# Attention by pairs of query tiles, with split values as stationary operand and results kept in DRAM

## The chip, the cores and the metric

The kernel runs on one core of a Trainium2 chip. The metric is the device time of one execution in microseconds. A core has five engines that run their own instruction lists and meet at semaphores: TensorE (PE: matmuls; its weight loads are shown as PEld), VectorE (DVE), ScalarE (ACT), GpSimd (POOL) and SyncE (SP, which here only issues transfers). Matmul results go to PSUM, eight banks of 128 partitions by 512 f32; everything else stands in SBUF.

## The reference, cut to what matters

One encoder layer over 2048 tokens of width 1024. The change touches the attention head group (8 heads) and how its result reaches the output projection. All is float32.

```python
q_rope = rope(q[..., 64:], cos, sin);  k_rope = rope(k_r, cos, sin)        # k_rope shared by the heads
s = einsum('bqhd,bkhd->bhqk', qn, k_nope) + einsum('bqhr,bkr->bhqk', qr, k_rope)
mask = key_chunk[None, :] <= q_chunk[:, None]                              # chunks of 64 tokens
p = softmax(where(mask, s * scale, -inf))
out = einsum('bhqk,bkhd->bqhd', p, v)                                      # (tokens, 8 heads x 64)
...
a = rms_norm(out, mla_out_g);  r = hgrn2_group(...)
h = layer_norm(ALPHA * x + concat([a, r]) @ w_out)
# then a mixture of 32 experts and a second layer norm
```

## The kernel before, in words

The program is a sequence of stages with a barrier between them: constants (phase_0), input projection and recurrence (phase_a), attention (phase_b), output projection with the first layer norm and router logits (phase_c), routing, experts, and the last layer norm. Within a stage every engine has a hand-written list, and semaphores with counted values set the order.

**Attention (phase_b, lines 639 to 870).** A loop over four pairs of heads (`pairs`, line 676); the first pass is written out, the other three are a hardware loop. A pass has two parts. First, twenty projections (`PREP`, line 672): k and q of both heads in four column chunks, and v in four. TensorE projects into the four S banks (lines 718, 721, 725), ScalarE copies k, the upper half of q, and v to SBUF (793, 795, 797), VectorE multiplies the rotary half of q by the trigonometric table (830). No attention work stands beside this part.

Then 32 items, one query tile of 128 rows for one head each (`ITEMS`), small and large tiles alternating. An item has q+1 key tiles, hence 1 to 4 banks (`BANKS`) of up to 512 scores. Its steps:
- scores, one f32 matmul per bank (769); an f32 matmul of these leaves two records in the trace
- row maximum per bank (845) with the masked corner written first (843), then over the banks (847), then negated and scaled (849), on VectorE
- exponential with the row sum accumulated (808), on ScalarE
- transposes of the probabilities, 128x128 each, up to four into one of two T banks (741); even banks are copied to SBUF by VectorE (859), odd ones by ScalarE (819)
- values: for each key tile one matmul with the transposed probabilities as stationary and 64 columns of v as moving operand (753)
- VectorE divides by the row sum and writes to `ao` in SBUF (865, 867, 870)

TensorE runs three items deep: in one turn it writes the scores of item n, then, group by group, the transposes of item n-1 and the values of item n-2. Nothing in a group's copy has to be ready before the next turn.

**Output projection (phase_c).** Eight steps of two token tiles. At the start of each step VectorE copies the next two tiles' attention results out of `ao` (`pick`, line 1113); ScalarE squares, sums and normalises them (1044 to 1054), TensorE transposes them into a single bank (985), ScalarE casts that to the rounded form `anT_hi` (1061), and VectorE subtracts to get the remainder `anT_lo` (1121).
## Time and profile before

| | us |
|---|---|
| median of 3 runs | 2902.32 (2900.85 to 2907.87) |
| the profiled execution | 2898.33 |
| its span | 2896.5 |
| TensorE / VectorE / ScalarE / GpSimd busy | 2587.7 / 1547.9 / 1076.9 / 308.8 |
| mean granted TensorE clock | 0.949 |

By stage (from the span's start): up to 823 us input projection and recurrence; 823 to 1618 attention; 1618 to 1872 output projection; then routing, experts from about 1985 to 2800, and the last norm. Busy time is the union of an engine's records. TensorE's are pipelined and their ends modelled, so a record is longer than its turn: how long a matmul holds TensorE is read from the distance between the starts of records that follow each other without a gap. The granted clock is the share of 2.4 GHz that TensorE was given; it has two levels, full and half. Where a line of the profile says `<-ACT pr L808 10.2`, the engine stood idle for 10.2 us in all until ScalarE's line 808 released it.

### The profile page before, as it was taken

To read this page: it belongs to the slowest core of one execution; us is meant where nothing else is said; L and a number is where in the kernel's file an instruction comes from. 1 tells how busy PE (TensorE), PEld (TensorE's weight loads), DVE (VectorE), ACT (ScalarE), POOL (GpSimd) and SP (SyncE) were. 2 spreads that over 40 slices of the span, in tenths; PEclk is the share of its full clock that TensorE was granted. 3 is DMA by queue.
4 is the path that set the end of the run, shared out by engine and by line. 5 is a ranking of instruction groups with operands and counts; after the bars stand their busy time and mean duration, and the time that the engine had idled before them with its cause. 6 is when DMAs were issued, how large, how long until landed. Compare 5 with 4: busy or idle time off the path is not lost. (4 is left out here: it accounts for less than half of the span.)

```text
span 2896.5 us, 42439 instructions
## 1 busy us (share of the span) xinstructions
PE 2587.7 (89%) x13160; PEld 2034.3 (70%) x13161; DVE 1547.9 (53%) x2657; ACT 1076.9 (37%) x1711; POOL 308.8 (11%) x221
## 2 busy tenths in 40 slices
PE   5999999999979999999989799937999999999960
PEld 4887788778837767667667578726877788888850
DVE  3334433343236546546456455465878775655738
ACT  2122222222134444344444322105666555545533
POOL 0000000000000000000000011100323332222215
PEclk9999999999979999999999899958999999999985
DMA  5000000000010000000000222257999997786935
GB/s 195 1 22 22 22 0 22 22 22 0 8 35 1 1 6 1 2 6 1 2 1 1 95 94 72 80 171 287 371 328 373 311 344 242 240 302 221 307 95 232
DMA packets 129115, 330.11 MB, mean 114 GB/s; under 512 B 7137, under 2 KB 19041, under 8 KB 128737
## 3 DMA queue, kind: packets, MB, share of 16 engines
q1 hardware_dynamic: 115904, 281.06, 26.4%
q0 software_dynamic: 13104, 47.72, 6.7%
q8 instruction: 57, 0.93, 0.1%
q14 instruction: 50, 0.40, 0.0%
HBM read 284.19 MB, written 53.48 MB: 117 GB/s over the span
## 5 line engine op out<-in xcount | busy, mean ns | idle before, releaser
L1582 DVE TENSOR_TENSOR w_raw<-w_raw,w_hi 128x4096 f32 (+1 forms) x96 | 424.5, 4422 | 149.2 <-ACT w_hi L1573 149.0
L1573 ACT CAST w_hi<-w_raw 128x4096 fp32r (+1 forms) x96 | 347.2, 3635 | 104.8 <-DMA w_raw<-in_w 93.8
L312 PE MATMUL pa<-xT,wi 128*128 128x256 f32 (+1 forms) x1536 | 335.6, 380 | 0.0
L808 ACT ACTIVATE pr<-pS,nmx 128x512 f32<-128x512 f32 (+3 forms) x320 | 195.7, 620 | 338.7 <-DVE nmx L849 328.0
L312 PEld LDWEIGHTS pa<-xT,wi 128*128 128x128 f32 (+1 forms) x1536 | 283.7, 186 | 53.9 <-issue 9.6
L1522 PE MATMUL eH<-w_hi,xh 128*128 128x512 f32 x720 | 290.6, 404 | 15.1 <-DVE xl L1640 15.1
L1523 PE MATMUL eH<-w_hi,xl 128*128 128x512 f32 x720 | 286.8, 398 | 0.0
L769 PE MATMUL pS<-kT,qT 128*128 128x512 f32 (+3 forms) x640 | 260.7, 539 | 12.2 <-ACT pr L808 8.4
L753 PE MATMUL pO<-vp,prT 128*128 128x64 f32 x2176 | 264.9, 271 | 0.0
L753 PEld LDWEIGHTS pO<-vp,prT 128*128 128x128 f32 x2176 | 259.6, 193 | 1.2 <-issue 1.2
L1092 POOL TENSOR_TENSOR hp<-hp,b 128x1024 f32<-128x1024 f32 x16 | 40.9, 2554 | 1812.0 <-DVE hp L1155 1812.0
L741 PE MATMUL pT<-ident,pr 128*128 128x128 f32 x1088 | 183.9, 291 | 42.4 <-ACT prT L819 25.2
L845 DVE TENSOR_REDUCE mx<-pS 128x1 f32<-128x512 f32 (+3 forms) x320 | 192.9, 609 | 45.5 <-PE pS L769 39.6
L741 PEld LDWEIGHTS pT<-ident,pr 128*128 128x128 f32 x1088 | 138.5, 155 | 87.9 <-ACT prT L819 25.6
L769 PEld LDWEIGHTS pS<-kT,qT 128*128 128x128 f32 x640 | 112.6, 193 | 108.7 <-issue 86.6
L1527 PE MATMUL eH<-w_raw,xh 128*128 x720 | 184.3, 398 | 4.6 <-DVE w_raw L1582 4.5
L1522 PEld LDWEIGHTS eH<-w_hi,xh 128*128 128x128 f32 x720 | 136.7, 190 | 47.5 <-issue 15.0
L1527 PEld LDWEIGHTS eH<-w_raw,xh 128*128 128x128 f32 x720 | 134.9, 188 | 40.2 <-issue 8.5
L601 DVE SCALAR_TENSOR_TENSOR state<-state,gf,pu 128x128 f32<-128x128 f32 x256 | 71.8, 342 | 164.4 <-PE po L425 146.2
L1541 PE MATMUL eY<-w_hi,uh 128*128 128x512 f32 x360 | 147.5, 410 | 13.0 <-ACT w_hi L1573 13.0
L1523 PEld LDWEIGHTS eH<-w_hi,xl 128*128 128x128 f32 x720 | 136.9, 190 | 31.3
L859 DVE COPY prT<-pT 128x512 f32<-128x512 f32 (+3 forms) x160 | 99.9, 624 | 88.4 <-PE pT L741 87.6
(271 smaller groups left out, 3873.5 us busy)
## 6 DMA issues: line engine op xcount, KB each, us to landing
w_raw<-in_w SPq DMA_DIRECT2D x96, 2048.0 KB, 13.1
xt<-in_x SPq DMA_DIRECT2D x8, 1024.0 KB, 5.6
wi<-in_w_in SPq DMA_DIRECT2D x4, 2048.0 KB, 17.3
xs<-in_x SPq DMA_DIRECT2D x8, 1024.0 KB, 4.9
scratch_h<-hp SPq DMA_DIRECT2D x16, 512.0 KB, 2.7
fz<-scratch_z SPq DMA_DIRECT2D x16, 512.0 KB, 9.7
out<-fz SPq DMA_DIRECT2D x16, 512.0 KB, 2.6
scratch_rT<-ot SPq DMA_DIRECT2D x8, 512.0 KB, 3.2
```

Of the source, the lines that this page charges most:

```text
L312: ins = pe.matmul(B[b][0:m_cols, 0:SPAN], wi[:, k, col:col + m_cols], xT[:, k, :], start=(k == 0), stop=(k == KT - 1))
L741: ins = pe.transpose(TB[u % 2][:, i * P:(i + 1) * P], pr[:, n % 2, kt_ * P:(kt_ + 1) * P], t["ident"][:])
L753: ins = pe.matmul(OB[n % 2][:, 0:VD], prT[:, n % 2, kt_, :], vp[:, kt_, x * VD:(x + 1) * VD], start=(kt_ == 0), stop=(kt_ == q))
L769: pe.matmul(S[u % 4][:, 0:w], qT[:, x, q * P:(q + 1) * P], kT[:, x, j * 512:j * 512 + w], start=True, stop=True).then_inc(s_done, 1)
L808: nc.scalar.activation(pr[:, n % 2, j * 512:j * 512 + w], S[u % 4][:, 0:w], ACT.Exp, scale=SCALE, bias=nmx[:, n:n + 1], accum_out=rsum[:, ...
L845: v.tensor_reduce(mx[:, n, j:j + 1], S[u % 4][:, 0:w], AX, ALU.max).then_inc(mx_part, 1)
L1522: pe.matmul(H[:], xh[:, k, :], w.hi[:, k, :], start=(k == 0), stop=False)
L1523: pe.matmul(H[:], xl[:, k, :], w.hi[:, k, :], start=False, stop=False)
L1527: ins = pe.matmul(H[:], xh[:, k, :], lo[:, k, :], start=False, stop=(k == KT - 1))
L1541: pe.matmul(Y[half][:], uh[:, k, :], w2.hi[:, k, at], start=(k == 0), stop=False)
L1573: nc.scalar.copy(w.hi[:], w.words(o).bitcast(F32)).then_inc(w.hi_ready, 1)
L1582: v.tensor_tensor(w.words(o), w.words(o).bitcast(F32), w.hi[:].bitcast(F32), ALU.subtract).then_inc(w.lo_ready, 1)
```

## The change

Attention is written anew. It now walks over 64 steps (`STEPS_B`): head by head, and in a head over eight pairs of query tiles, upward in even heads and downward in odd ones. Nothing is a loop any more; all is written out. A step has two halves, one for each query tile of the pair.
- q, k and v are kept as hi and lo. Scores are three split matmuls per bank (`score`).
- v's hi and lo stand side by side, 64 and 64 columns, as the stationary operand; the transposed probabilities of both query tiles, cast to hi by ScalarE (`cast`) and subtracted to lo by VectorE (`rest`), are the moving operand of 256 columns. A unit is two key tiles by two query tiles: four transposes into a bank and four matmuls (`weigh`), four units later (`LAG`), from a ring of six.
- The sum over a pair comes out as a transposed 128x256 block, the hi half over the lo half. ScalarE copies it (`copy_o`), and a small f32 matmul with a stacked identity both adds the halves and turns it back (`fold`), into one of the same two T banks. VectorE divides (`divide`), and SyncE stores it to DRAM.
- The projections of the next head are spread over pairs 0 to 3 of this one (`prep_in`), one chunk of k or q or v in a half. The rotary half of q now waits for ScalarE's copy of the upper half; then ScalarE casts the whole and VectorE subtracts.
- In the output projection, `pick` is gone: SyncE loads two tiles' attention results from DRAM, for the next step at the start of each. The norm's gain and bias are loaded there and no longer during attention.

```diff
+LAG, RING, FOLD_LAG = 4, 6, 2
...
+def prep_in(n, i):
+    h, q = STEPS_B[n]
+    if q > 3 or h + 1 == HEADS:
+        return []
...
-                                pe.matmul(S[u % 4][:, 0:w], qT[:, x, q * P:(q + 1) * P], kT[:, x, j * 512:j * 512 + w],
-                                          start=True, stop=True).then_inc(s_done, 1)
+                        pe.matmul(b[:, 0:w], qh[:, x, at], kh[:, x, keys], start=True, stop=False)
+                        pe.matmul(b[:, 0:w], ql[:, x, at], kh[:, x, keys], start=False, stop=False)
+                        pe.matmul(b[:, 0:w], qh[:, x, at], kl[:, x, keys], start=False, stop=True).then_inc(scored, 1)
...
+                def free_turn(e):
+                    if e >= NTB:
+                        kind, who = T_ORDER[e - NTB]
+                        if kind == "unit":
+                            pe.wait_ge(t_lo, who + 1)
+                        else:
+                            pe.wait_ge(a_ready, who + 1)
+                    return T[e % NTB]
...
-                            ins = pe.matmul(OB[n % 2][:, 0:VD], prT[:, n % 2, kt_, :], vp[:, kt_, x * VD:(x + 1) * VD],
-                                            start=(kt_ == 0), stop=(kt_ == q))
+                    for m, (kk, w) in enumerate(((0, ph), (1, ph), (1, pl), (0, pl))):
+                        narrow = kk == 1 and g == q
+                        o = out[:, P:2 * P] if narrow else out
+                        at = slice(2 * P, 3 * P) if narrow else slice(kk * 2 * P, (kk + 1) * 2 * P)
+                        ins = pe.matmul(o, v[:, 2 * g + kk], w[:, u % RING, at], start=(g == 0 and m == 0), stop=(g == q and m == 3))
...
+                def fold(n):
+                    pe.wait_ge(o_copied, n + 1)
+                    b = free_turn(T_AT["fold", n])
+                    for i in range(2):
+                        ins = pe.matmul(b[:, i * VD:(i + 1) * VD], oT[:, n % 2, i * P:(i + 1) * P], t["fold"][:, 0:VD], start=True, stop=True)
...
+                for n in range(NI + 2):
+                    for i in range(2):
+                        if n < NI:
+                            score(n, i)
+                            for p in prep_in(n, i):
+                                project(p)
+                        for s in slots_in(n, i):
+                            if s < NU:
+                                turn(s)
+                            if LAG <= s < NU + LAG:
+                                weigh(s - LAG)
+                            if s in FOLD_SLOT:
+                                fold(FOLD_SLOT[s])
...
+                        for k in range(max(len(slots), pieces)):
+                            if k < len(slots):
+                                if slots[k] < NU:
+                                    cast(slots[k])
+                                if slots[k] in COPY_SLOT:
+                                    copy_o(COPY_SLOT[slots[k]])
+                            if k < pieces:
+                                exp(n, i, k)
+                            if k == 0 and n < NI:
+                                for p in prep_in(n, i):
+                                    copy_q(p) if p[0] == "q" else split(p)
...
+                        if n < NI:
+                            peak(n, i)
+                            for p in prep_in(n, i):
+                                rope(p) if p[0] == "q" else split(p)
+                        for s in slots_in(n, i):
+                            if s < NU:
+                                rest(s)
+                            if s in FOLD_SLOT:
+                                divide(FOLD_SLOT[s])
...
 # phase_c
+                sp.dma_start(ap[:], ad[0]).then_inc(a_loaded, 16)
...
+                    if not last:
+                        sp.wait_ge(a_norm, m * 2 + 2)
+                        sp.dma_start(ap[:], ad[m + 1]).then_inc(a_loaded, 16)
...
-                    v.tensor_scalar(ap[:], t["ao"][:, bass.ds(m * 2, 2), :], 1.0, None, ALU.mult).then_inc(a_picked, 1)
...
-                    if not last:
-                        pick(m + 1)
```

TensorE's list before, at an item of two banks between a larger and a smaller one (pS scores, pT transposes, pO values):

```order
L769 MATMUL pS<-kT,qT 128x512
L769 MATMUL pS<-kT,qT 128x384
L741 MATMUL pT<-ident,pr 128x128 x4
L753 MATMUL pO<-vp,prT 128x64 x4
L741 MATMUL pT<-ident,pr 128x128 x4
L753 MATMUL pO<-vp,prT 128x64 x2
L741 MATMUL pT<-ident,pr 128x128 x3
```

and now, in a large pair, the last score matmul of one half, its first and last unit, and the next half's first scores (k_hi and k_lo, q_hi and q_lo, prT_hi and prT_lo are the parts of the split):

```order
L825 MATMUL pS<-k_lo,q_hi 128x384
L843 MATMUL pT<-ident,pr 128x128 x4
L863 MATMUL pO<-prT_hi,v_split 128x256 x2
L863 MATMUL pO<-prT_lo,v_split 128x256 x2
...
L843 MATMUL pT<-ident,pr 128x128 x4
L863 MATMUL pO<-prT_hi,v_split 128x256
L863 MATMUL pO<-prT_hi,v_split 128x128
L863 MATMUL pO<-prT_lo,v_split 128x128
L863 MATMUL pO<-prT_lo,v_split 128x256
L823 MATMUL pS<-k_hi,q_hi 128x512
L824 MATMUL pS<-k_hi,q_lo 128x512
```

Scores are three matmuls where one stood, and a half's units stand behind its scores, each with four transposes and, for an earlier unit, four wide value matmuls.

VectorE's list before, for one item of four banks (mx, mxa, nmx the maxima; rsa, rin the row sums):

```order
L845 TENSOR_REDUCE mx<-pS 128x1 x3
L843 MEMSET pS 64x64
L845 TENSOR_REDUCE mx<-pS 128x1
L847 TENSOR_REDUCE mxa<-mx 128x1
L849 TENSOR_SCALAR nmx<-mxa 128x1
L859 COPY prT<-pT 128x384
L865 TENSOR_REDUCE rsa<-rsum 128x1
L867 RECIPROCAL rin<-rsa 128x1
L870 TENSOR_SCALAR ao<-pO,rin 128x64
```

and now, for a half of a small pair in which q and v of the next head are projected, and the maxima of the half behind it:

```order
L1016 TENSOR_REDUCE mxa<-mx 128x1
L1018 TENSOR_SCALAR nmx<-mxa 128x1
L985 TENSOR_TENSOR q_raw<-pS,trig 64x512
L1002 TENSOR_TENSOR v_split<-pS,v_split 128x4x64 x2
L1023 TENSOR_TENSOR prT_lo<-pT,prT_hi 128x512
L1023 TENSOR_TENSOR prT_lo<-pT,prT_hi 128x384
L994 TENSOR_TENSOR q_lo<-q_raw,q_hi 128x512
L1014 TENSOR_REDUCE mx<-pS 128x1
L1012 MEMSET pS 64x64
L1014 TENSOR_REDUCE mx<-pS 128x1
L1016 TENSOR_REDUCE mxa<-mx 128x1
L1018 TENSOR_SCALAR nmx<-mxa 128x1
```

Between one half's maxima and the next's stand the subtraction of every unit (prT_lo), and around these the rotary product, v's remainder and q's remainder. ScalarE's list alternates a unit's cast with an exponential, and the pieces of the next head stand behind the first exponential of a half.

In the output projection, VectorE at the border of two steps before:

```order
L1117 TENSOR_TENSOR rts_lo<-rts,rts_hi 128x512
L1101 COPY hT<-cH 128x512
L923 UNCONDITIONAL_BRANCH
L923 ISA
L1113 ISA
L1113 TENSOR_SCALAR ap<-ao 128x1024
L1120 ISA
L1121 TENSOR_TENSOR anT_lo<-cA,anT_hi 128x512
```

and now:

```order
L1342 TENSOR_TENSOR hp<-hp,g 128x1024
L1306 TENSOR_TENSOR rts_lo<-rts,rts_hi 128x512
L1296 COPY hT<-cH 128x512
L1111 UNCONDITIONAL_BRANCH
L1111 ISA
L1310 TENSOR_TENSOR anT_lo<-cA,anT_hi 128x512
```

The copy `ap<-ao` between the last copy of a step and the first anT_lo of the next is gone.

## Rows read from the trace of the kernel before

**Rows 1.** The page: engines' busy time; one row of its transfers.
```profile
PE 2587.7 (89%) x13160; PEld 2034.3 (70%) x13161; DVE 1547.9 (53%) x2657; ACT 1076.9 (37%) x1711; POOL 308.8 (11%) x221
...
scratch_h<-hp SPq DMA_DIRECT2D x16, 512.0 KB, 2.7
```

**Rows 2.** Busy by stretch: PE, PEld, DVE, ACT, POOL, granted clock, DMA share, GB/s.
```profile
858.00:1050.00 192.00, 178.53 (x1036) 130.09 (x1037) 107.03 (x320) 80.27 (x219) 0.00 (x0) 0.97 0.01 3
...
1240.00:1430.00 190.00, 173.94 (x1044) 128.24 (x1042) 104.72 (x318) 78.77 (x217) 0.00 (x0) 0.98 0.01 4
```

**Rows 3.** Who waited for whom, 860 to 1610: total us, times, longest.
```profile
ACT pr L808 <- DVE nmx L849: 325.4, 116, 5.7
```

**Rows 4.** Groups by shape, attention: busy us, mean ns, idle before and releasers.
```profile
L753 PE MATMUL pO<-vp,prT 128*128 128x64 f32 x2176 | 264.9, 271 | 0.0
...
L769 PE MATMUL pS<-kT,qT 128*128 128x512 f32 x448 | 213.8, 603 | 0.0
L741 PE MATMUL pT<-ident,pr 128*128 128x128 f32 x1088 | 183.9, 291 | 42.4 <-ACT prT L819 25.2 <-ACT pr L808 10.2 <-DVE prT L859 6.7
```

**Rows 5.** Timelines of TensorE: start, length of the run, records (x).
```profile
706.93 1.99 PE L320 MATMUL pa<-xT,wi 128*128 128x256 f32 x8
...
839.99 14.00 PE L721 MATMUL pS<-cqn,wq 128*128 128x512 f32 x32
853.83 3.73 PE L725 MATMUL pS<-wv,ckvn 128*128 128x128 f32 x32
...
1204.00 0.60 PE L741 MATMUL pT<-ident,pr 128*128 128x128 f32 x4
1204.43 1.00 PE L753 MATMUL pO<-vp,prT 128*128 128x64 f32 x8
```

**Rows 6.** Timeline of TensorE in the experts: split matmuls.
```profile
1999.81 0.40 PE L1542 MATMUL eY<-w_hi,ul 128*128 128x512 f32 x1
2000.04 0.40 PE L1541 MATMUL eY<-w_hi,uh 128*128 128x512 f32 x1
```

**Rows 7.** Timeline of VectorE and ScalarE, an item of two banks.
```profile
1209.29 0.69 DVE L845 TENSOR_REDUCE mx<-pS 128x1 f32<-128x512 f32 x1
1210.01 0.15 DVE L847 TENSOR_REDUCE mxa<-mx 128x1 f32<-128x2 f32 x1
1210.20 0.15 DVE L849 TENSOR_SCALAR nmx<-mxa 128x1 f32<-128x1 f32 x1
...
1210.39 0.69 ACT L808 ACTIVATE pr<-pS,nmx 128x512 f32<-128x512 f32 x1 [2.67 <-DVE nmx L849]
...
1211.07 0.68 ACT L808 ACTIVATE pr<-pS,nmx 128x512 f32<-128x512 f32 x1
...
1212.76 1.31 DVE L845 TENSOR_REDUCE mx<-pS 128x1 f32<-128x512 f32 x2
```

**Rows 8.** Timeline of ScalarE at the start of attention: two copies.
```profile
825.30 1.06 ACT L785 COPY kT<-pS 64x512 f32<-64x512 f32 x2 [15.19 <-PE pS L703]
```

**Rows 9.** Busy by stretch, end of the output projection.
```profile
1850.00:1900.00 50.00, 36.21 (x186) 31.45 (x184) 20.90 (x44) 5.82 (x12) 7.52 (x3) 0.79 0.28 101
```

**Rows 10.** Output projection: timeline around one step's start; its wait in total.
```profile
1703.10 2.18 DVE L1113 TENSOR_SCALAR ap<-ao 128x1024 f32 x1
...
1705.20 0.68 DVE L1121 TENSOR_TENSOR anT_lo<-cA,anT_hi 128x512 fp32r<-128x512 f32 x1
1706.03 0.63 PE L985 MATMUL cA<-ident,an 128*128 128x128 f32 x4 [1.68 <-DVE anT_lo L1121]
...
PE cA L985 <- DVE anT_lo L1121: 14.3, 7, 3.5
```

**Rows 11.** Timeline of the output projection's first load and the cast it releases.
```profile
1618.66 0.39 SPq L930 DMA_DIRECT2D rts<-scratch_rT  x1
...
1622.20 1.14 ACT L1031 CAST rts_hi<-rts 128x512 fp32r<-128x512 f32 x2 [5.89 <-DMA rts<-scratch_rT]
```

More of the change, by code:

```diff
@@ L116, in shape_constants @@
     fold[:64, 64:] = (s[:64, None] % 32 == s[None, :64] % 32)
+    fold[:, :64] = (s[:, None] % 64 == s[None, :64])
     c["fold"] = fold
@@ L639, in phase_b @@
+S_ORDER = bank_order()
+S_AT = {e: n for n, e in enumerate(S_ORDER)}
+T_ORDER = [e for s in range(SLOTS + 1) for e in ([("unit", s)] if s < NU else []) + ([("fold", FOLD_SLOT[s])] if s in FOLD_SLOT else [])]
+T_AT = {e: n for n, e in enumerate(T_ORDER)}
+NTB = 2
 def phase_b(nc, t, d):
@@ new lines, in phase_b @@
+        qraw = sb("q_raw", [P, 2, 512])
+        pr = [t["krp"]] + [sb(f"pr{i}", [P, SEQ]) for i in range(3)]
+        ph = sb("prT_hi", [P, RING, 512], F32R); pl = sb("prT_lo", [P, RING, 512], F32R)
+        oT = sb("oT", [P, 2, 2 * P])
+        a = sb("a_out", [P, 4, 2, VD])
+        mx = sb("mx", [P, 4, 4])
+        mxa = sb("mxa", [P, 2 * NI])
+        nmx = sb("nmx", [P, 2 * NI])
+        rsum = sb("rsum", [P, 2 * NI, 4])
+        rin = sb("rin", [P, 2 * NI])
+        S = [psum(f"pS{i}") for i in range(4)]
@@ new lines, in peak @@
+                def peak(n, i):
+                    tile, pieces, part = 2 * n + i, PIECES[n][i], EXP_AT[n][i]
+                    for j in range(pieces):
+                        b, w = S[S_AT["score", (n, i, j)] % 4], width(n, i, j)
+                        v.wait_ge(scored, part + j + 1)
+                        if j == pieces - 1:
+                            v.memset(b[0:64, w - 64:w], -3.0e38).then_inc(masked, 1)
+                            v.wait_ge(masked, tile + 1)
+                        v.tensor_reduce(mx[:, tile % 4, j:j + 1], b[:, 0:w], AX, ALU.max).then_inc(mx_part, 1)
+                    v.wait_ge(mx_part, part + pieces)
+                    v.tensor_reduce(mxa[:, tile:tile + 1], mx[:, tile % 4, 0:pieces], AX, ALU.max).then_inc(mx_all, 1)
+                    v.wait_ge(mx_all, tile + 1)
+                    v.tensor_scalar(nmx[:, tile:tile + 1], mxa[:, tile:tile + 1], -SCALE, None, ALU.mult).then_inc(nmx_ready, 1)
```

468 lines of the change are left out of this document (269 added, 199 removed).

## The prediction

> **What bounds the kernel now.** I read the page first, then the stages, then the attention stage (lines 703 to 870) by shapes and waits. The profiled execution took 2898.3 us, 1.8 more than its span; the median of the runs is 2902.3, so what I add to the one I add to the other. TensorE is busy 89% of the span, VectorE 53%, ScalarE 37% [rows 1]. The change touches two stages: attention, from 823 to about 1618 us, 795 us long, and the output projection behind it, to about 1872 [rows 2]. In one of attention's four head pairs TensorE's records cover 174 of 190 us, VectorE's 105, ScalarE's 79 [rows 2]. ScalarE waits 325 us for the negated maximum [rows 3], while TensorE's largest wait, before transposes, is 42 us in all [rows 4].
>
> TensorE's own work there goes by the distance from one record to the next, not by their length, since records overlap [rows 5]: an f32 matmul leaves two records, of 0.432 us at 512 columns (31 distances in 14.00-0.59), 0.229 at 256, 0.112 at 128 and 0.107 at 64; a transpose leaves one, 0.11 us. With the counts of the shapes (the three largest in [rows 4]; the others follow from the loops):
> - scores 448x0.432 + 64x(0.325+0.229+0.112) = 236 us (0.325 for 384 columns lies between its neighbours)
> - probabilities times values 2176x0.107 = 233
> - transposes 1088x0.11 = 120
> - projections 128x0.432 + 64x0.432 + 128x0.112 = 97, rotary fold 6
>
> That is 692 us of 795; the other 103 are waits, gaps and low clock.
>
> **What the change makes of that work.** Each score piece becomes three split matmuls. A warm split matmul of 512 columns follows the next after 0.23 us, 0.234 over the longer run they stand in [rows 6]; none narrower is in the trace. Bounds for 256 columns: half the distance, 0.117, and the f32 pair, 0.458. I take 0.127, the row's 0.020 over its streaming kept, because the row is the same kind of instruction. For 384 I take 0.18; for 128 the bounds are 0.06 and 0.224, and I take 0.22, the f32 row of that very width, on the side of caution (it moves the sum by 35 us at most).
> - scores 672x0.234 + 96x(0.18+0.127+0.22) = 208 (was 236)
> - values: 288 units of four matmuls, of which 128 have 128 columns: 1024x0.127 + 128x0.22 = 158 (was 233)
> - transposes 120, projections 97, rotary fold 6: as before
> - new: 128 folds of hi and lo, f32, 64 columns, 2x0.107 each = 27
>
> Sum 616: TensorE is relieved of 76 us. The bounds of the unknown widths (for 384, up to the f32 pair's 0.65) make this 570 to about 1030.
>
> The other two pay. Before, 160 groups of probabilities were copied by VectorE and 160 by ScalarE. Now each of 288 units is cast by ScalarE and then subtracted by VectorE: 128 more casts at about 0.53 and 128 more VectorE passes at about 0.62. Also new are the hi and lo of q, k and v. VectorE's sum goes from some 430 (four pairs like those of [rows 2]) to about 560, ScalarE's from 330 to 480. Neither becomes the bound by its sum; the order is what costs.
>
> **The new waits.** Turned probabilities have only two PSUM banks and each unit's bank is freed by the second engine in series. I follow the rounds, one round being half a pair of query tiles. VectorE's step costs in a chain: 0.62 per 512 piece, then mask, last reduction, mxa and nmx 0.15+0.72+0.19+0.19 = 1.25; exp to exp 0.68 [rows 7]; copies back to back 0.48 for two of 0.58 in 1.06 us [rows 8], 0.53 for casts; the next engine starts about 0.03 after a record's end, TensorE 0.15 after (1705.88 to 1706.03 in [rows 10]).
> - Long rounds (pairs 4 to 7, 64 of them). With four pieces and four units: scores 4x3x0.234 = 2.81, first transposes 0.63 until seen, cast 0.53, exp 0.68, cast 0.59, subtraction 0.69, 0.15 to TensorE, fourth transposes 0.44, values 0.51: 7.03. Once per pair ScalarE's copy of O and VectorE's division (0.15+0.17+0.28 and their own gaps) stand in this chain, 0.45 per round: 7.5. TensorE's work in it with its share of folds is 6.8. Over the 64, TensorE's work is 5.6 on average (18.6 scores, 24.7 units, 1.7 folds per head, by eight rounds); I add 0.9: 6.55x64 = 419.
> - Short rounds that project a piece of k for the next head (28): VectorE's circle is peak 1.55 (half a 0.62, and 1.25), exp 0.71, ScalarE's k_hi 0.58, 0.03, k_lo 0.69, subtractions 0.80, division 0.4: 4.8, against some 3.1 of TensorE. 134.
> - Those that project q (16): 1.55, 0.71, copy 0.51, rotary product 0.72, subtractions 0.80, q_lo 0.62, division 0.6: 5.5, 88. With v as well (12): two casts and two subtractions of 256 columns and 0.9 of projection more, 8.0, 96.
> - Short rounds of the last head (8) 3.2 each, 26; rotary fold and head 0's twelve projections 27; the end 5.
>
> Sum 795 us: the waits grow from 103 to 179 and eat TensorE's relief exactly. What hid the copies before, a whole query tile of scores and values between a transpose and its use, has become four units.
>
> **The clock.** Attention was granted 0.97 and 0.98 in the pairs shown [rows 2]. At the end of the output projection, with records over 36 of 50 us and longer pauses, it was 0.79 [rows 9]. A share of 0.88 means that a quarter of the time passes at 1.2 instead of 2.4 GHz. With 616 us of work in 795, I estimate 0.88 in place of 0.97. TensorE's links are 4.4 of a 7.5 us chain, so 250 us of the long rounds plus 20 at the start stretch by a tenth: +25, between 0 and the 60 of a clock of 0.79. By the Trainium skill, TensorE: Matmul & The Clock Gate, Part 4 on PE-mode transposes, transposes do not count as TensorE activity in the same way as matmuls. By that, the 120 us of transposes, now a larger part of less work, help the clock less than the records suggest; no row here separates them. With that rule the term lies nearer 60 than 0.
>
> **The ends.** The results go to DRAM, and the stage waits for the last store: a 512 KB store lands in 2.7 us [rows 1], so +3; the other 63 stores have nobody behind them but the same output buffer four pairs later. The output projection loses its copy of attention results out of SBUF, 2.18 us of VectorE in the loop. It stood between the end of a step and anT_lo, for which TensorE waited 14.3 us in 7 steps [rows 10]: -13. The new load of the next two tiles waits on SyncE behind the store of the tile before, a few us into a step, and lands some 3.5 us later (as rts does, 1618.66 to 1622.20 in [rows 11]), and the normalisation is wanted at the next step, some 20 us later: hidden. SyncE's queue gets a_norm in front, which is a step old by then. The first load stands behind rts, whose landing starts the stage: up to 1 us more. The gain and bias loads move behind x, used only after the last wo_lo, about 1642: hidden.
>
> **Sum.** Profiled: 2898.3 + (795-795) + 25 + 3 - 13 = 2913; as a median, 2917 us, 0.5% slower.
>
> **Rivals.**
> - Even. The clock holds at 0.97 (the pauses are single microseconds): 2917-25 = 2892. For it: pauses of this length stand in attention now, with 0.97. Against it: there are more of them.
> - Faster: the rounds overlap better than my chains. TensorE runs up to its LAG of four units ahead, so that waits stay at today's 103: attention 719, total 2902-76-13+3 = 2816; with half of that 2860. For it: TensorE is the fullest engine, and every other sum is below 616. Against it: two banks, not six ring slots, limit the transposes, and every q passes ScalarE, VectorE, ScalarE, VectorE.
> - Slower: the weight loads of the split matmuls show. An f32 matmul of 64 columns takes 0.107 per record, though its share of the 512-column row is 0.054 [rows 5], so loads do bound narrow ones. If at 256 columns a load of some 0.10 stood beside the stream, 0.207 each: 1024x0.080 = +82 of work, of which the loops' idle 0.9 a round absorbs a third: 2917+55 = 2972. It decides from the point where the 256-column distance passes 0.14. A clock of 0.8 throughout gives about 2950 by another way. The Trainium skill, same page, section on LDWEIGHTS, puts a load at columns over 1.2, in ns: an estimate of 107 ns for 128 columns, just what streaming 256 columns takes here, so hiding is just possible by it.
> - Split matmuls under 512 columns run at the f32 pair's speed: 1120x0.331 = 371 more work, and the waits hide a fourth of it at most: near 3200.
>
> **How the numbers follow.** A difference under 0.3%, 9 us, is what measuring can't tell from none. My forecast, 2895 to 2945, has 0.37: faster 0.03, same 0.08, slower 0.26. Even, 0.25: 0.12, 0.10, 0.03. Faster, 0.25, all faster. Slower, 0.10, and the f32 speed, 0.03, all slower. Sum: faster 0.40, same 0.18, slower 0.42. The range leaves out the f32 speed and half of the faster rival: 2835 to 2975.
>
> **What would show it.** Attention's length, 795 now: 820 forecast. Per step: the distance of 256- and 128-column split matmuls; TensorE's idle time before transposes ended by VectorE's prT_lo, and before scores ended by ScalarE's exp; rounds of 7.5 us in pair 7 and 5 to 8 in pairs 0 to 3; the granted clock; no wait of cA for anT_lo. It is wrong if TensorE's waits for prT_lo and exp stay near today's, if the clock stays at 0.97, or if VectorE is seen working without a gap.

## The result

The changed kernel takes **2921.0 us**, the median of 7 runs (2913.8 to 2924.8); the kernel before took 2902.6 us (7 runs, 2899.0 to 2907.9). The ratio is 1.0057, with a 95% interval of 1.0041 to 1.0073: slower by 18 us, 0.6%. The forecast was 2917 us, in a range of 2835 to 2975. The profiled execution took 2924.2 us, 2922.4 of them its span, against 2898.3 before.

The two changed stages can be bounded by events: attention begins with TensorE's first matmul of the stage, at 823.3 us before and at 825.7 now, and SyncE issues the output projection's first load when attention's results have been stored. (The words ahead of the prediction let the output projection end near 1872; TensorE's last matmul for the logits, cL, starts at 1890.1.)

```profile
825.73 7.06 PE L774 MATMUL pS<-krp,fold 64*64 64x512 f32 x8 [13.94 <-PEq L630]
```

| | before | after | forecast of the difference |
|---|---|---|---|
| all ahead of attention (unchanged code) | 823.3 us | 825.7 us | 0 |
| attention, from there to that load | 795.3 us (to 1618.66) | 811.9 us (to 1637.59) | +28 |
| output projection, to the last cL | 271.4 us (to 1890.1) | 268.8 us (to 1906.4) | -13 |
| all that follows (unchanged code) | 1008 us | 1018 us | 0 |
| profiled execution | 2898.3 | 2924.2 | +15 |

The 2.4 us ahead of attention and the last 10 us belong to no edit: the text of the stages there is the same. Most of it is the scatter of single executions: in the traces of the experiments below, attention began between 822.8 and 829.1 us, and all that follows took 1005 to 1017 us. The profile of before also lies 4 us under the median of its kernel, and that of after 3 us over. For the change itself +16.5 and -2.6 us remain, 14 of the 18.4 us between the medians.

### The profile page after: what moved, and what is told of

The parts are those of the page before. It is cut to its first block and busy times, and to the rows that moved or that the text cites. A ratio compares the mean times of both kernels' runs of the same rounds, so it can differ in the third digit from the quotient of the medians.

```text
span 2922.4 us, 41381 instructions
## 1 busy us (share of the span) xinstructions
PE 2533.2 (87%) x12712; PEld 2028.5 (69%) x12713; DVE 1640.9 (56%) x2690; ACT 1184.5 (41%) x1951; POOL 317.2 (11%) x221
## 5 line engine op out<-in xcount | busy, mean ns | idle before, releaser
L935 ACT CAST prT_hi<-pT 128x512 fp32r<-128x512 f32 (+1 forms) x288 | 161.9, 562 | 264.9 <-PE pT L843 264.9
L1023 DVE TENSOR_TENSOR prT_lo<-pT,prT_hi 128x512 fp32r<-128x512 f32 (+1 forms) x288 | 187.7, 656 | 100.0 <-ACT prT_hi L935 99.8
L1014 DVE TENSOR_REDUCE mx<-pS 128x1 f32<-128x512 f32 (+2 forms) x320 | 188.8, 607 | 16.8 <-PE pS L825 10.9
L843 PE MATMUL pT<-ident,pr 128*128 128x128 f32 x832 | 158.2, 283 | 37.6 <-DVE prT_lo L1023 36.2
L927 ACT ACTIVATE pr<-pS,nmx 128x512 f32<-128x512 f32 (+1 forms) x240 | 153.3, 641 | 53.0 <-DVE nmx L1018 50.4
L843 PEld LDWEIGHTS pT<-ident,pr 128*128 128x128 f32 x832 | 104.6, 146 | 65.5 <-issue 41.7
L1729 PE MATMUL eY<-w_hi,ul 128*128 128x512 f32 x360 | 144.1, 400 | 0.0
L823 PE MATMUL pS<-k_hi,q_hi 128*128 128x512 f32 (+2 forms) x320 | 129.1, 403 | 13.2 <-ACT pr L927 11.2
L863 PE MATMUL pO<-prT_hi,v_split 128*128 128x256 f32 x576 | 138.6, 323 | 0.0
## 6 DMA issues: line engine op xcount, KB each, us to landing
fz<-scratch_z SPq DMA_DIRECT2D x16, 512.0 KB, 10.7
```

The source lines that it names most:

```text
L843: ins = pe.transpose(b[:, m * P:(m + 1) * P], probs(n, i)[:, kt * P:(kt + 1) * P], t["ident"][:])
L927: nc.scalar.activation(probs(n, i)[:, j * 512:j * 512 + w], S[S_AT["score", (n, i, j)] % 4][:, 0:w], ACT.Exp, scale=SCALE, bias=nmx[:, til ...
L935: nc.scalar.copy(ph[:, u % RING, 0:w], T[T_AT["unit", u] % NTB][:, 0:w]).then_inc(t_hi, 1)
L1014: v.tensor_reduce(mx[:, tile % 4, j:j + 1], b[:, 0:w], AX, ALU.max).then_inc(mx_part, 1)
L1023: v.tensor_tensor(pl[:, u % RING, 0:w], T[T_AT["unit", u] % NTB][:, 0:w], ph[:, u % RING, 0:w].bitcast(F32), ALU.subtract).then_inc(t_lo, 1)
```

## The profile after

The page of the changed kernel, busy time and share first; then three groups (busy us, mean ns, idle time before them and who ended it). It answers to [rows 1] and [rows 4].

```profile
PE 2533.2 (87%) x12712; PEld 2028.5 (69%) x12713; DVE 1640.9 (56%) x2690; ACT 1184.5 (41%) x1951; POOL 317.2 (11%) x221
...
L935 ACT CAST prT_hi<-pT 128x512 fp32r<-128x512 f32 (+1 forms) x288 | 161.9, 562 | 264.9 <-PE pT L843 264.9
L1023 DVE TENSOR_TENSOR prT_lo<-pT,prT_hi 128x512 fp32r<-128x512 f32 (+1 forms) x288 | 187.7, 656 | 100.0 <-ACT prT_hi L935 99.8
...
L843 PE MATMUL pT<-ident,pr 128*128 128x128 f32 x832 | 158.2, 283 | 37.6 <-DVE prT_lo L1023 36.2
```

TensorE has 448 records less and is 54 us less busy, VectorE 93 us more, ScalarE 108 us more. The waits have changed hands. Before, ScalarE waited 325 us for the negated maximum [rows 3]; now its largest wait is for transposes, and TensorE's largest is for the subtraction. (Two names, pr and krp, stand for the buffers of probabilities in these rows: one of the four buffers is the tile that held the rotary part of k.) The view of who waited for whom, 825 to 1600 us (total, times, longest):

```profile
ACT prT_hi L935 <- PE pT L843: 256.1, 138, 7.0
DVE prT_lo L1023 <- ACT prT_hi L935: 92.8, 147, 1.3
DVE q_raw L985 <- ACT q_raw L917: 79.9, 32, 5.1
...
PE pT L843 <- DVE prT_lo L1023: 60.7, 89, 2.6
ACT pr L927 <- DVE nmx L1018: 47.0, 54, 2.8
...
DVE k_lo L997 <- ACT k_hi L906: 36.1, 28, 2.1
```

With the wait ahead of the folds (30.2 us in 36, of the same releaser), TensorE waits 91 us for VectorE's remainder; before, its waits for the copies that empty a turn bank came to 25.2 + 6.7 us [rows 4]. This is a circle: a turn bank is filled by four transposes, cast by ScalarE, subtracted from by VectorE, and only then free, and there are two such banks.

The pitch of the split matmuls, which the forecast had to bound, is read from starts. Three stretches of TensorE's timeline: score pieces of 512 and 384 columns, of 128, and one unit with its first and last transpose, its four value matmuls and the next unit's first transpose:

```profile
1332.64 0.39 PE L825 MATMUL pS<-k_lo,q_hi 128*128 128x512 f32 x1
1332.87 0.33 PE L823 MATMUL pS<-k_hi,q_hi 128*128 128x384 f32 x1
1333.04 0.34 PE L824 MATMUL pS<-k_hi,q_lo 128*128 128x384 f32 x1
...
1157.74 0.22 PE L823 MATMUL pS<-k_hi,q_hi 128*128 128x128 f32 x1
1157.80 0.28 PE L824 MATMUL pS<-k_hi,q_lo 128*128 128x128 f32 x1
1157.91 0.28 PE L825 MATMUL pS<-k_lo,q_hi 128*128 128x128 f32 x1
...
1340.68 0.27 PE L843 MATMUL pT<-ident,krp 128*128 128x128 f32 x1
...
1341.00 0.27 PE L843 MATMUL pT<-ident,pr 128*128 128x128 f32 x1
1341.03 0.48 PE L863 MATMUL pO<-prT_hi,v_split 128*128 128x256 f32 x2
1341.35 0.40 PE L863 MATMUL pO<-prT_lo,v_split 128*128 128x256 f32 x2
1341.59 0.27 PE L843 MATMUL pT<-ident,krp 128*128 128x128 f32 x1
```

So 512 columns take 0.23 us, 384 take 0.17, and 128 take 0.11, half of the 0.22 assumed. Only the first of three 128-column matmuls, behind one of 512, is followed sooner, after 0.06 (1157.74 to 1157.80). 256 columns take 0.11 to 0.12 (three starts at 1164.59, 1164.70 and 1164.82). A whole unit, four transposes and four value matmuls, takes 0.91 us (1340.68 to 1341.59); the first value matmul follows the last transpose after 0.03 us, and the third follows the first after 0.32.

Where the clock is low is seen by stretches (PE, PEld, DVE, ACT, POOL, clock, DMA share, GB/s). Each cycle of two heads has a long part, large pairs, and a short part, in which the next head's q, k and v are made. The first row is a long part, the second a short one; the bounds are starts of VectorE's divisions, a_out:

```profile
1102.00:1195.00 93.00, 82.84 (x558) 72.91 (x557) 70.22 (x163) 61.00 (x160) 0.00 (x0) 1.00 0.04 11
1195.00:1306.00 111.00, 84.61 (x385) 58.43 (x384) 60.74 (x164) 46.20 (x120) 0.00 (x0) 0.85 0.02 5
```

The 0.97 of before [rows 2] has become 1.00 in the long part and 0.85 in the short one. What the engine did before it fell, in such a short part (timeline; in brackets the idle time before, and who ended it):

```profile
1076.56 0.44 PE L863 MATMUL pO<-prT_lo,v_split 128*128 128x128 f32 x2
1079.67 1.27 DVE L1023 TENSOR_TENSOR prT_lo<-pT,prT_hi 128x512 fp32r<-128x512 f32 x2
1080.49 1.09 PE L870 MATMUL pT<-fold,oT 128*128 128x64 f32 x4 [3.48 <-DVE prT_lo L1023]
...
1082.76 0.63 PE L823 MATMUL pS<-k_hi,q_hi 128*128 128x512 f32 x1
1083.19 0.63 PE L824 MATMUL pS<-k_hi,q_lo 128*128 128x512 f32 x1
...
1094.23 1.09 PE L843 MATMUL pT<-ident,pr 128*128 128x128 f32 x4 [2.33 <-DVE prT_lo L1023]
```

TensorE stood 3.5 us for the remainder, and the matmuls behind it follow each other after 0.43 us instead of 0.23: that is the level of 1.2 GHz, and a pause is paid twice. It needs none of the longest: only three of TensorE's pauses in attention exceed 3 us, and behind the 2.33 us before 1094.23 the transposes are slow as well (four in 1.09 us, 0.63 at the full clock).

For the experiments one row of each kernel suffices, the whole of attention. Before and after:

```profile
825.00:1616.00 791.00, 730.35 (x4215) 528.28 (x4214) 425.21 (x1276) 329.02 (x888) 0.00 (x0) 0.97 0.02 5
```

```profile
825.00:1635.00 810.00, 673.28 (x3784) 522.92 (x3784) 532.00 (x1320) 435.56 (x1129) 0.00 (x0) 0.92 0.03 8
```

The part in which no matmul record runs grew from 61 to 137 us (791-730, 810-673). In later rows the same 3784 matmuls cover less time at a higher clock, so such a row parts a gain into pauses (the difference of the first two numbers) and, in the main, clock (the second number). Not all of the second number is clock: between the kernel with three edits and the last run it falls from 634 to 615 us at the same 0.98.

## The experiments

**Theory T**: the added waits come from the circle through two turn banks, with the rotary product of q and its clock as a second loss and the new load of attention's results as a third. **R1**: TensorE's work, or other waits, set the time, and a third bank adds little.

### Three turn banks

The eight PSUM banks are divided into 4 for scores, 3 for turned probabilities and 1 for outputs, in place of 4, 2 and 2; a pair's first value matmul then waits for the copy of the pair before.

```
-NTB = 2
+NTB = 3
...
-        O = [psum(f"pO{i}")[:, 0:2 * P] for i in range(2)]
+        O = [psum("pO")[:, 0:2 * P]] * 2
...
-                    if g == 0 and n >= 2:
-                        pe.wait_ge(o_copied, n - 1)
+                    if g == 0 and n >= 1:
+                        pe.wait_ge(o_copied, n)
```

> The changed kernel with three PSUM banks for turned probabilities instead of two; the bank is taken from the output sums, which now share one. Theory (T): attention's lost time is the wait for the second engine in series to free one of two banks. In the changed kernel TensorE waits 63 us before transposes and 31 us before folds for VectorE's prT_lo, 94 in all, and ScalarE waits 265 us for transposes. With a third bank most of the 94 go and some of it is taken back by other waits: attention 812 -> 750 to 765 us, total 2921 -> 2865 to 2880, TensorE's wait for prT_lo under 30 us. Rival (R1, engines' work): VectorE and ScalarE are simply loaded with more; the order of banks does not matter: total within 9 us of 2921. Rival (R2, clock): the low clock of 0.92 is the cause, the banks only through it: total falls by less than 25 us and only where the clock rises.

Measured: 2833.6 us (2826.8 to 2837.3), ratio to the kernel before 0.9759 (0.9745 to 0.9773), 87 us less than the changed kernel, and more than either reading expected. Attention as a whole, then its long and short part:

```profile
825.00:1550.00 725.00, 643.11 (x3781) 498.41 (x3780) 523.62 (x1318) 432.37 (x1129) 0.00 (x0) 0.96 0.04 9
...
1071.00:1158.00 87.00, 82.81 (x559) 72.40 (x559) 69.48 (x167) 60.60 (x162) 0.00 (x0) 1.00 0.05 12
1158.00:1249.00 91.00, 73.82 (x389) 49.86 (x388) 60.26 (x165) 46.25 (x121) 0.00 (x0) 0.98 0.03 7
```

and TensorE's wait for the remainder (825 to 1600):

```profile
PE pT L848 <- DVE prT_lo L1028: 11.7, 24, 0.8
```

Attention is 85 us shorter: 55 of it pauses (137 to 82) and 30 the same matmuls at the higher clock (673 to 643). The wait ahead of transposes fell from 60.7 to 11.7 us, its longest from 2.6 to 0.8, and the one ahead of folds from 30.2 to 1.2. The long part loses 6 us of 93, the short part 20 of 111. The expectation had the pauses about right; theory T left out the clock, and R2, which named it, allowed less than 25 us.

### One output bank alone

The same, with the two turn banks kept: this parts the third turn bank from what was given up for it.

> Control for the run with three banks: the changed kernel with the output sums in one bank and the turned probabilities still in two. A pair's first value matmul must then wait for ScalarE's copy of the pair before. Theory T: this costs up to 10 us and gains nothing, 2921 to 2931. If the run with three banks gained because of something else in that edit, this one would gain as well.

Measured: 2919.3 us (2915.1 to 2923.4), ratio 1.0053 (1.0037 to 1.0069). No difference from the changed kernel: the whole 87 us belong to the third turn bank.

### The rotary product of q without its wait

VectorE's product of q with the cosines waited for ScalarE's copy of q's other half, which is needed only by the cast behind both. The wait is moved to that cast.

```
-                    v.wait_ge(q_copied, Q_AT[m] + 1)
                     v.tensor_tensor(qraw[64:128, ...], S[...][64:128, :], t["trig"][64:128, ...], ...)
...
+                        act.wait_ge(q_copied, Q_AT[m] + 1)
                         act.wait_ge(q_roped, Q_AT[m] + 1)
```

> The changed kernel with VectorE's rotary product no longer waiting for ScalarE's copy of q's upper half (the cast of the whole q waits for both). In the changed kernel VectorE stood 79.9 us before this product in 32 places. Theory T (short rounds are a chain ScalarE, VectorE, ScalarE, VectorE): the product moves in front of the copy and half a microsecond of each of the 28 chains goes, with the exponential before it in some: 10 to 30 us less, 2891 to 2911. Rival R1 (the wait covers TensorE's projection anyway): under 6 us, VectorE then waits for the projection instead.

Measured: 2885.0 us (2878.3 to 2886.4), ratio 0.9933 (0.992 to 0.9945), 36 us less than the changed kernel, more than the 10 to 30 expected. Attention, then its long and short part:

```profile
825.00:1600.00 775.00, 646.90 (x3783) 506.56 (x3781) 531.79 (x1319) 435.11 (x1129) 0.00 (x0) 0.96 0.03 8
...
1087.00:1180.00 93.00, 82.84 (x558) 72.84 (x557) 70.31 (x163) 60.98 (x160) 0.00 (x0) 1.00 0.04 11
1180.00:1281.00 101.00, 76.52 (x385) 52.91 (x383) 60.57 (x163) 45.79 (x119) 0.00 (x0) 0.93 0.03 6
```

VectorE's wait for that copy is gone; a part of it comes back further on, since its wait ahead of v's remainder grew from 12.1 to 41.8 us. The long part is untouched, as it must be, since no q is made there; the short part is 10 us shorter. Of the 35 us that attention lost, only 9 are pauses (137 to 128) and 26 are clock (673 to 647). An edit that takes single microseconds out of a few pauses was worth almost four times that, and most of it is the engine's higher level.

### The load one tile earlier

In the output projection, the load of the next two tiles of attention results waits behind the store of the tile before. It is issued ahead of that store instead, late in the step before.

```
-                    if not last:
-                        sp.wait_ge(a_norm, m * 2 + 2)
-                        sp.dma_start(ap[:], ad[m + 1]).then_inc(a_loaded, 16)
...
+                            if more:
+                                sp.wait_ge(a_norm, m * 2 + 4)
+                                sp.dma_start(ap[:], ad[m + 2]).then_inc(a_loaded, 16)
```

> The changed kernel with the output projection's load of attention results issued half a step earlier on SyncE, ahead of the store of the second tile. In the changed kernel ScalarE waited 27.6 us for this load in 7 steps, VectorE's reciprocal 37.5 us behind it, and the reciprocal stands in VectorE's list before the residual sum; TensorE still waited 10.7 us for anT_lo. Theory T: that late load is where the predicted 13 us went: 8 to 12 us less, TensorE's wait for anT_lo under 3 us, ScalarE's wait for the load near 0. Rival: TensorE's own work bounds the step and the load is hidden: within 3 us, anT_lo still waited for.

Measured: 2913.1 us (2904.3 to 2917.5), ratio 1.0036 (1.0023 to 1.005), 8 us less, at the lower edge of the 8 to 12 expected; the interval still overlaps the changed kernel's, so the trace has to decide. First the changed kernel; this step of the output projection begins at 1723.7, with VectorE's anT_lo:

```profile
1726.39 0.37 SPq L1133 DMA_DIRECT2D ap<-scratch_a  x1
...
1730.02 0.63 ACT L1238 ACTIVATE an<-ap 128x512 f32<-128x512 f32 x1 [4.23 <-DMA ap<-scratch_a]
...
1731.86 0.17 DVE L1315 RECIPROCAL ars<-ars 128x2 f32<-128x2 f32 x1 [5.34 <-ACT ars L1243]
...
1732.14 1.28 DVE L1330 SCALAR_TENSOR_TENSOR hp<-xs,cM 128x512 f32<-128x512 f32 x2
```

The load is issued 2.7 us into the step and is used 3.6 us later. In ScalarE's list the normalisation for the next step stands right behind this step's two casts, done at 1725.8, so ScalarE waits for it from then on, VectorE's reciprocal (ars) waits for ScalarE, and the residual sum (hp), for which TensorE's results had been ready, stands behind the reciprocal in VectorE's list. With the early load (issued at 1720.08) ScalarE's wait falls from 27.6 us in 7 to 0.6 in 1, and the stage takes 262.1 us (1639.97 to 1902.1) against 268.8. TensorE's wait for anT_lo is 6.2 us in 2, not the under 3 that was expected.

### All three

> The changed kernel with all three edits: three banks for transposed probabilities and one for outputs, the rotary half without its wait, the output projection's load issued one tile earlier. Theory T (three separate losses: the turn banks 87 us, the rotary multiply 36, the load 8, the first two sharing a part of the rising clock): 2785 to 2815 us, waits of TensorE in attention under 80 us, clock there 0.96 to 0.98. Rival R1 (the banks' gain already holds the rotary's, since both filled the same idle time): 2820 us or more.

Measured: 2806.8 us (2799.8 to 2811.3), ratio 0.9667 (0.9652 to 0.9682), 114 us less than the changed kernel and 3.3% under the kernel before; alone the three gave 87, 36 and 8. Attention:

```profile
825.00:1529.00 704.00, 633.75 (x3783) 492.81 (x3781) 524.22 (x1319) 431.66 (x1129) 0.00 (x0) 0.98 0.04 9
```

So this run's rival falls, though of the rotary edit's 36 us only some 19 (114-87-8) come on top of the banks'. The pauses are down to 70 us, near those of the kernel before (61), for less work.

### One score matmul instead of three

```
-                        pe.matmul(b[:, 0:w], qh[:, x, at], kh[:, x, keys], start=True, stop=False)
-                        pe.matmul(b[:, 0:w], ql[:, x, at], kh[:, x, keys], start=False, stop=False)
-                        pe.matmul(b[:, 0:w], qh[:, x, at], kl[:, x, keys], start=False, stop=True).then_inc(scored, 1)
+                        pe.matmul(b[:, 0:w], qh[:, x, at], kh[:, x, keys], start=True, stop=True).then_inc(scored, 1)
```

> Each score bank gets one matmul instead of three (the two with a remainder are left out), everything else as in the changed kernel; about 125 us of TensorE's attention work is gone. Theory T (rounds last as long as the chain copy, subtraction, value matmuls, next turn on two banks): most of it turns into waiting, 5 to 40 us less than the changed kernel, 2880 to 2916 us. Rival R2 (TensorE's work sets the attention): 100 us less or more, 2820 us or below.

Measured: 2901.9 us (2894.9 to 2905.0), ratio 1.0002 (0.9993 to 1.0011). A sixth of the stage's matmuls, 640, are left out, and the kernel gains 19 us:

```profile
825.00:1617.00 792.00, 582.62 (x3143) 433.42 (x3141) 527.04 (x1319) 436.36 (x1129) 0.00 (x0) 0.88 0.03 8
...
1094.00:1188.00 94.00, 71.19 (x462) 60.87 (x462) 70.24 (x167) 61.20 (x161) 0.00 (x0) 0.93 0.04 11
```

The pauses grew from 137 to 209 us and the clock fell from 0.92 to 0.88. The long part lasts 94 us with one matmul for a piece, and 93 with three. TensorE's amount of work, though it is the fullest engine of the page, does not set the length of attention in the changed kernel.

### No remainders of the probabilities

VectorE's subtraction is left out, and the two value matmuls that use its result; a turn bank is free after the cast.

```
-                            pe.wait_ge(t_lo, who + 1)
+                            pe.wait_ge(t_hi, who + 1)
...
-                    for m, (kk, w) in enumerate(((0, ph), (1, ph), (1, pl), (0, pl))):
+                    for m, (kk, w) in enumerate(((1, ph), (0, ph)) if g else ((0, ph), (1, ph))):
```

> The remainders of the transposed probabilities are left out: no subtraction on VectorE (188 us busy) and two of the four value matmuls of each unit (about 70 us of TensorE work), everything else as in the changed kernel. Theory T (the subtraction stands in the loop that holds a turn bank): 100 to 160 us less, 2760 to 2820 us, more than the run with one score matmul although less TensorE work is gone. Rival R2 (TensorE's work sets the attention): 50 to 75 us less, 2845 to 2870 us, and less than that run gains.

Measured: 2779.6 us (2776.7 to 2780.6), ratio 0.9573 (0.9559 to 0.9588): 141 us less, with 576 matmuls fewer, each narrower than most of the 640 of the run above. Set beside it, this says which work lies in the circle: with the subtraction out as well, less TensorE work removed buys seven times as much. The run alone doesn't part a bank that is free sooner from a VectorE that has less to do; the third bank, with VectorE's work unchanged, does.

### The kernel before with three turn banks

Does the old kernel gain by the same division of banks? It too had two turn banks, each emptied by one copy of one engine.

```
-        TB = [psum(f"pT{i}") for i in range(2)]
-        OB = [psum(f"pO{i}") for i in range(2)]
+        TB = [psum(f"pT{i}") for i in range(3)]
+        OB = [psum("pO")] * 2
...
```

> The kernel before with the same division of banks: three for transposed probabilities, one for outputs. Its two turn banks are each emptied by one copy of one engine, without a subtraction. Theory T (the rewrite made the loop through a turn bank long; before it was short): 0 to 25 us less than the kernel before, 2878 to 2903 us, so that the rewrite is worth 40 us or more once both have three banks. Rival R3 (two turn banks held back the kernel before as much): 50 us less or more, 2850 us or below.

Measured: 2875.9 us (2869.8 to 2877.4), ratio 0.9903 (0.9887 to 0.9918), 25 us less than before, at the edge of the 0 to 25 expected; its attention takes 768.2 us (829.06 to 1597.22) instead of 795.3, 27 less. With three turn banks on either side the rewrite is the faster kernel, by 42 us (2833.6 to 2875.9); with two it is the slower one, by 18.

### The wait for the remainder moved behind the first two value matmuls

```
-                    pe.wait_ge(t_lo, u + 1)
                     for m, (kk, w) in enumerate(((0, ph), (1, ph), (1, pl), (0, pl))):
+                        if m == 2:
+                            pe.wait_ge(t_lo, u + 1)
```

> As the run with all three edits (2807 us), but TensorE begins a unit's two value matmuls with the rounded probabilities when the copy is there, and waits for VectorE's remainder only ahead of the other two. With three turn banks the wait ahead of a unit's value matmuls is the first that needs this unit's remainder, so it can move. Theory T: what is left of TensorE's waits for the remainder shrinks, 5 to 25 us less, 2782 to 2802 us. Rival R4 (TensorE's own work and the softmax's passes now set the attention): 2800 to 2814 us.

> The same later wait put into the changed kernel as it is, with two turn banks. Theory T (the turn that stands ahead of a unit's value matmuls reuses this unit's bank, so it has already waited for the same remainder): no difference, 2913 to 2926 us. Rival R1 (the value matmuls' own wait costs the time, not the bank): 15 us less or more, 2906 us or below.

Measured: 2808.0 us (2801.6 to 2809.4) in the kernel with three edits, nothing gained, as R4 said and against T; and 2919.3 us (2911.2 to 2921.7) in the changed kernel, ratio 1.0051 (1.0033 to 1.0069), no difference, as T said. The wait ahead of the value matmuls is never the late one: the wait before transposes is 11.7 us in 24 in the run with three edits and in this one alike. So something else holds up what is left.

### What is left: one score matmul, and a shorter maximum

> One score matmul instead of three (the two with a remainder are left out) in the kernel with all three edits. With two turn banks this was worth 19 us. Theory T (with the waits gone TensorE's work and its clock set more of the attention): 40 to 90 us less than the 2807 of the same kernel with three, 2717 to 2767 us. Rival R5 (the attention still hangs on the engines' chains, and less work only lowers the granted clock): under 30 us less, 2777 us or above.

Measured: 2814.6 us (2809.6 to 2822.5), ratio 0.9706 (0.9681 to 0.9731). Theory T failed: nothing is gained. Attention:

```profile
825.00:1538.00 713.00, 556.60 (x3143) 410.54 (x3141) 524.44 (x1320) 430.93 (x1129) 0.00 (x0) 0.93 0.04 9
```

TensorE's wait for a score bank, 825 to 1500, here and in the run with the three edits and all three matmuls:

```profile
PE pS L825 <- ACT pr L931: 50.6, 81, 1.6
```

```profile
PE pS L825 <- ACT pr L933: 10.6, 26, 1.0
```

The work taken from TensorE turned into waiting for the exponential that frees a score bank, and the clock fell from 0.98 to 0.93. This points to a second circle: score bank, maximum, negated maximum, exponential, bank free. The last run shortens VectorE's pass in it:

```
-                        v.tensor_reduce(mx[:, tile % 4, j:j + 1], b[:, 0:w], AX, ALU.max).then_inc(mx_part, 1)
+                        v.tensor_reduce(mx[:, tile % 4, j:j + 1], b[:, 0:64], AX, ALU.max).then_inc(mx_part, 1)
```

> The kernel with all three edits (2807 us), but VectorE's pass over a score bank takes its maximum from the first 64 columns only: the same instructions in the same order, some 0.45 us shorter each, 320 of them, about 140 us of VectorE in attention. A softmax needs no exact maximum, so the computation stands but for its safety with large scores. Theory C (what is left, also with one score matmul, is the circle score bank, maximum, negated maximum, exponential, bank free again): 40 to 110 us less, 2700 to 2767 us. Rival R6 (TensorE's work, whose records cover 634 of 704 us, sets the attention): under 30 us less, 2777 us or above.

Measured: 2755.7 us (2750.9 to 2756.4), ratio 0.9498 (0.9482 to 0.9514), 51 us less than the kernel with three edits, and the fastest that was run. Its maxima, as a group, and then its attention by the view of stretches:

```profile
L1019 DVE TENSOR_REDUCE mx<-pS 128x1 f32<-128x64 f32 x320 | 68.1, 220 | 27.2 <-PE pS L827 22.7
```

```profile
825.00:1480.00 655.00, 615.22 (x3783) 491.49 (x3781) 412.36 (x1320) 424.81 (x1129) 0.00 (x0) 0.98 0.04 10
```

118 us less of VectorE (186 to 68) shortened attention by 50 us, while a sixth of TensorE's matmuls less had shortened it by nothing. The result lies where theory C had it. VectorE also frees the turn banks, and it has 118 us less to do in all, so this run does not part a shorter circle of score banks from an earlier subtraction or a less loaded VectorE: C is supported, not shown, and that stays open.

## Why the prediction was nearly right, point by point

- **TensorE's work, 616 us.** Some 34 us too high. The 128-column score pieces take 0.11, not 0.22: 96 x 0.11 = 11 us less. In back-to-back units (0.91 us) the four transposes and four value matmuls cost 0.04 less than the 0.95 assumed, over 288 units another 11. The 128 narrow value matmuls, put at 0.22 against 0.127 for wide ones, take no longer than these: 12 more. About 582 us at full clock, an estimate. The guess for 256 columns, 0.127, was the one on which most hung (1024 matmuls), and it held within 0.01 to 0.02.
- **The rival of unhidden weight loads, 2972, and that of f32 speed, near 3200.** Both are out: the first decided from a pitch above 0.14 at 256 columns, and the rows have 0.11 to 0.12. The narrow matmuls do show a floor, 0.11 us for 128 columns as for 256 where they follow one another. The Trainium skill (TensorE: Matmul & The Clock Gate, section on LDWEIGHTS) puts a load at the columns over 1.2, in ns, an estimate of 107 ns for 128. The trace agrees with that page, and not with the rival, which let the load stand beside the stream.
- **The waits grow and eat the relief.** Right in mechanism, and shown by experiment: the third turn bank returned 87 us, the giving up of an output bank nothing. The prediction named it, "two banks, not six ring slots, limit the transposes", as what speaks against the faster rival. A long round of four pieces was to last 7.5 us; scores start at 1330.71 and those of the next half at 1337.93, 7.2 us. The sizes are less right. Attention's 812 us less the 582 of work leave 230 us of waits, gaps and low clock, where the forecast had 207 (179, 25 and 3). Work too high by 34 and waits too low by 23 partly cancel inside one term. The other two engines' work was overstated as well: VectorE had 532 us in attention against 560, ScalarE 436 against 480.
- **The clock.** +25 us for 0.88; measured 0.92. The same matmuls cover 673 us at 0.92, 643 at 0.96 and 634 at 0.98 (three edits), so against the 0.97 of before the clock costs some 35 us, an estimate. The size was near; the place was wrong. The prediction put the stretch on the long rounds, which ran at 1.00. It falls in the short ones (0.85), behind pauses like those of 2.33 and 3.48 us above. The long rounds ran at 1.00 though up to four transposes stand in every unit of 0.91 us, so nothing here bears out the rule of the Trainium skill (same page, Part 4) on transposes, by which the prediction would have moved the term towards 60.
- **The ends of attention.** The last result is divided out at 1635.1 and the load goes at 1637.59: 2.5 us, against 0.5 before (1618.11 to 1618.66), when nothing had to be stored: +2, near the forecast (3).
- **The output projection, -13, measured -2.6.** This is the step that failed: "the normalisation is wanted at the next step, some 20 us later: hidden." That the load goes a few us into a step was right (2.7). But the next step's normalisation is wanted early in the same step, 0.6 us before the load is even issued, and in VectorE's list its reciprocal stands ahead of the residual sum. The wait that was to vanish (14.3 us in 7, [rows 10]) is 10.7 us in 8. The early load gets 6.7 us of it back (268.8 to 262.1), and with it the stage is 9.3 us shorter than before, near the 13 of the forecast.
- **The sum.** +15 forecast for the profiled execution, +26 measured, +14 of it in the changed stages: attention 11.5 us better than the +28, the output projection 10 us worse than the -13. Two misses of opposite sign, and a third pair inside attention: the closeness of 2917 to 2921 is in good part luck.
- **The even rival, 2892, and the faster one, 2816 or 2860.** The clock did not hold, so the first is out. The second describes a kernel one edit away: with three turn banks the pauses fall to 82 us and the time to 2834. What decides between it and the forecast could have been read ahead: a turn bank is held for its transposes, 0.44, the cast, 0.56, and the subtraction, 0.66, in series, 1.66 us without the hand-overs; by two banks 0.83 per unit, only 0.08 under TensorE's 0.91, which the hand-overs take (to TensorE alone the prediction had 0.15 per unit, by two banks 0.08); by three 0.55.

## What to carry to other kernels

When a second engine is put in series on a buffer, count the time that one buffer is held and the number of buffers before counting the work that is saved: here what the forecast counted as 76 us of saved TensorE work became 18 us of loss, and one bank, given up elsewhere at no cost, turned that into 69 us of gain. The Trainium skill (Perfetto Trace Analysis, section Identifying Performance Opportunities) says that the same gap repeating on the engine that should be saturated can mean too few buffers for the next tile; this case shows it with 89 waits of up to 2.6 us that fell to 24 of up to 0.8. The same section says to optimize the most-contended engine first, and to look for what its gaps wait for. Only the second helped here: 640 matmuls less on TensorE were worth 19 us with two turn banks and nothing with three, while following its waits found the 87 us. A cheap test of what sets a stage is therefore to leave out a part of the fullest engine's work and look at the length of a round, before optimizing that work.

## What the hardware showed that was not expected

- A pause is paid twice. Taking VectorE's wait before the rotary product (79.9 us in 32) out of the short rounds shortened TensorE's pauses by 9 us and the matmuls themselves by 26 us, and the clock of a short part rose from 0.85 to 0.93.
- Less work on TensorE can lower its clock: with a third of the score matmuls the clock of attention went from 0.92 to 0.88, and from 0.98 to 0.93 in the kernel with three edits, where nothing was gained (2806.8 and 2814.6, the ranges 2799.8 to 2811.3 and 2809.6 to 2822.5 overlapping).
- Split matmuls of 128 and of 256 columns that follow one another have nearly the same pitch, 0.11 to 0.12 us. Four value matmuls of which two have 128 columns take as long as four of 256 (1162.00 to 1162.54, and 1158.41 to 1158.96), so narrowing these below 256 columns saves nothing. Three score matmuls of 128 columns behind one of 512 take 0.29 us (1157.74 to 1158.03), three of 256 take 0.36 (1164.59 to 1164.95).
